# mLSTM rows by tile: denominators of four heads at once, and banks handed back before the statistics

## What is computed

```python
# for each of two directions d, per token j and head h:
den = s.sum(-1) + inter * einsum('bhck,bhcjk->bhcj', n_in, qc)
h   = num / maximum(abs(den), exp(-m_j))[..., None]
hx[0] + hx[1]                                    # both directions are added
(h - mu) * rsqrt(var + eps), merged, * ml_norm_w # then gated by sigmoid(o)
# attention: softmax(q k + bias, and q k over the context), times v
```

## Time and profile before

| | |
|---|---|
| median of 3 runs | 4099.18 us (4097.99 to 4102.63) |
| the profiled execution | 4098.68 us, of which its span is 4096.5 us |
| TensorE busy | 3561.6 us, 87% of the span |
| VectorE busy | 2733.5 us, 67% |
| rows and turns of layer 0 | from 363.56 us to about 472 us |
| rows and turns of layer 1 | from 2632.48 us |

### The profile page before, as it was taken

How to read it: one execution, slowest core, us unless ns; L and a number is a source line. 1 busy time by engine, 2 the same in 40 slices (tenths; PEclk the granted TensorE clock), 3 DMA queues, 4 the chain that set the end, 5 groups by cost and what they waited for, 6 DMA issues and landing times.

```text
span 4096.5 us, 46129 instructions
## 1 busy us (share of the span) xinstructions
PE 3561.6 (87%) x12012; PEld 1542.5 (38%) x12012; DVE 2733.5 (67%) x6918; ACT 1712.1 (42%) x4825; POOL 1846.6 (45%) x1405
## 2 busy tenths in 40 slices
PE   7998999888888888897888987899988888888887
PEld 3445654433333333333211221565433333333332
DVE  3106677677777777777766665768767777777775
ACT  2013534444444444444444443444444444444443
POOL 1111025556556555554433433104545655655555
PEclk9999999999999999999999999899999999999999
DMA  7653559999999999999999998658999999999998
GB/s 277 243 182 97 187 209 421 421 421 421 416 420 418 410 418 411 418 419 415 415 418 410 412 413 329 175 200 346 421 422 422 421 420 416 417 415 415 413 420 335
DMA packets 252758, 1503.73 MB, mean 367 GB/s; under 512 B 25888, under 2 KB 53024, under 8 KB 81808
## 3 DMA queue, kind: packets, MB, share of 16 engines
q0 software_dynamic: 193536, 1393.97, 83.4%
q1 hardware_dynamic: 59024, 107.45, 7.6%
HBM read 1494.91 MB, written 2.21 MB: 365 GB/s over the span
## 4 chain that ended last, share of the span: by engine, by line
DMA 44%; PE 27%; DVE 8%; issue 8%; ACT 7%; POOL 4%; SPq 1%; POOLq 0%; DVEq 0%; ACTq 0%
DMA arena<-in_updown,arena 44%; PE psum L1258 8%; POOL arena L1914 4%; DVE arena L2464 4%; PE psum L1201 3%; PE psum L1043 3%; PE psum L1059 2%; PE psum L1346 2%; ACT arena L1682 1%; PE psum L1071 1%; ACT arena L1678 1%; ACT L1748 1%; PE psum L1228 1%; ACT L1667 1%; PE psum L914 1%
## 5 line engine op out<-in xcount | busy, mean ns | idle before, releaser
L1914 POOL DMA_INDIRECT arena<-in_updown,arena x1280 | 1752.8, 1369 | 1751.3 <-PE psum L1258 845.4
L1258 PE MATMUL psum<-arena 128*128 128x512 f32 x4096 | 1998.0, 617 | 336.9 <-ACT arena L1682 320.2
L2464 DVE CUSTOM_DVE_ANT_0 arena<-arena 128x1024 bf16<-128x1024 f32 x1276 | 1566.0, 1227 | 901.3 <-DMA arena<-in_updown,arena 797.3
L1258 PEld LDWEIGHTS psum<-arena 128*128 128x128 f32 x4096 | 714.6, 191 | 1391.2 <-ACT arena L1682 826.5
L1748 ACT ACTIVATE arena<-arena 128x1 f32<-128x1 f32 x1280 | 259.1, 202 | 1663.1 <-DVE arena L2464 1660.2
L1682 ACT ACTIVATE arena<-CN,arena 128x128 f32<-128x128 f32 x1280 | 513.9, 402 | 44.9
L1678 ACT ACTIVATE arena<-arena 128x1 f32<-128x1 f32 x1280 | 376.7, 294 | 66.9 <-ACT arena L1748 3.9
L1346 PE MATMUL psum<-arena 64*64 64x512 f32 x2048 | 294.3, 647 | 117.9 <-ACT arena L1682 116.9
L1228 PE MATMUL psum<-arena 128*128 128x256 f32 (+1 forms) x1280 | 364.0, 385 | 3.0 <-ACT arena L1653 1.6
L1228 PEld LDWEIGHTS psum<-arena 128*128 128x128 f32 x1280 | 239.6, 191 | 260.6 <-issue 252.0
L1346 PEld LDWEIGHTS psum<-arena 64*64 64x64 f32 x2048 | 54.9, 136 | 306.8 <-ACT arena L1682 280.7
(11 more groups left out here) (266 smaller groups left out, 2644.6 us busy)
## 6 DMA issues: line engine op xcount, KB each, us to landing
arena<-in_ada_w POOLq DMA_DIRECT2D x40, 1024.0 KB, 5.7
arena<-in_updown,arena POOLq DMA_INDIRECT x1280, 14.7
arena<-in_wq SPq DMA_DIRECT2D x16, 1024.0 KB, 18.4
arena<-in_w_in SPq DMA_DIRECT2D x50, 256.0 KB, 7.3
arena<-in_w_in SPq DMA_DIRECT2D x5, 2048.0 KB, 12.8
arena<-in_w_in SPq DMA_DIRECT2D x17, 512.0 KB, 5.3
arena<-in_ada_w SPq DMA_DIRECT2D x4, 2048.0 KB, 14.2
arena<-in_consts SPq DMA_DIRECT2D x16, 512.0 KB, 5.7
```

The costliest lines, as they stand in the source:

```text
L1258: mm = e.matmul(ps[ACCUMULATORS[t % 2][hf]][:], diag[:, k % DIAGS, :], ring[k % RING][:, D + hf * 512:D + (hf + 1) * 512], start=first, st ...
L1914: e.indirect_dma_start(ring[k % RING], None, updown, bass.IndirectOffsetOnAxis(ap=idx16[:, k:k + 1], axis=0)).then_inc(sem(f"rows{k % RING ...
L2464: e.tensor_tensor_reduce(prod[:, k % 2, :], ring[k % RING][:, 0:D], u, 1.0, 0.0, ALU.mult, ALU.add, dots[:, k:k + 1]).then_inc(sem("expert ...
```

## The change

1. VectorE works by tile. `denominators(j)` waits until all four heads of tile j are in PSUM and does floor, maximum and reciprocal for four heads in one instruction each (three instead of eight). `head_rows(j, c)` adds up two heads' rows, `head_stats(j)` takes the four statistics of the tile afterwards.
2. The banks are handed back earlier: a new semaphore `mixer.sums_read` rises after the last reading of each pair of banks, ahead of the statistics. TensorE's group g waits for its value g - 1 (the same group g - 2). `keep_clock` and the turns wait for it too.
3. The first pairs' scores stand elsewhere: `scores(0)` after group 1, `scores(1)` after group 3 (both stood after group 2). Their maxima stand ahead of the last tile's denominators (they stood between its two groups), the divisions of pair 0 between its two halves of rows.
4. `no_bias` moves to other memory and is written before the rows; two of the eight bias blocks use a second block of zeros, `late_zeros`, which VectorE writes at p = 4 of the turns, after the wait for `mixer.bands_placed` that stood ahead of the first maxima.
5. Two semaphores of GpSimd (`ahead.ctx_copied`, `eps_set`) become one, with the counts adapted.

The diff, cut to its core:

```diff
@@ TensorE
-                        e.wait_ge(sem("mixer.h_done"), 2 * g - 2)
+                        e.wait_ge(sem("mixer.sums_read"), g - 1)
...
                 for g in range(2 * (NT - t0)):
                     head_sums(g)
-                    if g == 2:
+                    if g == 1:
                         e.wait_ge(sem("mixer.w_ready"), NT - t0)
-                        scores(0)
-                        scores(1)
+                    if g in (1, 3):
+                        scores(g // 2)
...
-                e.wait_ge(sem("mixer.h_done"), MLH * (NT - t0) - 2)
+                e.wait_ge(sem("mixer.sums_read"), 2 * (NT - t0) - 1)
                 keep_clock(ps[4], 3)
@@ VectorE
+                def denominators(j):
+
+                    e.wait_ge(sem("mixer.num_ready"), MLH * (j - t0 + 1))
+                    dn = psum[:, 4:4 + MLH, DV:2 * DV + 2:DV + 1]
...
+                    ch.link(e.scalar_tensor_tensor(out=den[:, MLH:2 * MLH, :], in0=dn, scalar=-1.0, in1=floor, op0=ALU.mult, op1=ALU.max))
+                    ch.link(e.tensor_tensor(den[:, 0:MLH, :], dn, den[:, MLH:2 * MLH, :], ALU.max))
+                    ch.link(e.reciprocal(rden[:], den[:, 0:MLH, :]))
+
+                def head_rows(j, c):
+
+                    heads = (2 * c, 2 * c + 1)
+                    for h in heads:
+                        ins = e.tensor_scalar(H[:, j, h * DV:(h + 1) * DV], psum[:, 4 + h, 0:DV], rden[:, h, 0:1], None, ALU.mult)
                     ch.link(ins)
+                    for h in heads:
+                        w = H[:, j, h * DV:(h + 1) * DV]
+                        ins = e.scalar_tensor_tensor(out=w, in0=psum[:, 4 + h, DV + 1:2 * DV + 1], scalar=rden[:, h, 1:2], in1=w, op0=ALU.mult, op1=ALU.add)
+                    ins.then_inc(sem("mixer.sums_read"), 1)
+
+                def head_stats(j):
+
+                    e.wait_ge(sem("mixer.sums_read"), 2 * (j - t0 + 1))
+                    for h in range(MLH):
+                        ins = e.bn_stats(bns[:, h, :], H[:, j, h * DV:(h + 1) * DV])
                     ch.link(ins)
...
+                    for h in range(MLH):
+                        e.bn_aggr(stat[:, j * MLH + h, :], bns[:, h, :]).then_inc(sem("mixer.h_done"), 1)
...
+                e.memset(no_bias, 0.0)
+                for j in range(t0, NT):
+                    if j == NT - 1:
+                        find_max(0)
+                        find_max(1)
+                    denominators(j)
+                    head_rows(j, 0)
+                    if j == NT - 1:
                         normalise(0)
                         normalise(1)
...
+                    head_rows(j, 1)
+                    head_stats(j)
+                    if j > t0:
+                        shift(j - 1)
                 for p in range(2, len(pairs) + 3):
...
+                    if p == 4:
+                        e.wait_ge(sem("mixer.bands_placed"), 16 * BAND_DMAS)
+                        ch.link(e.memset(late_zeros, 0.0))
```

More of the change, by code:

```diff
@@ L575, in build @@
         probT = [r(512) for _ in range(JOB_SLOTS - 1)] + [Region(ARENA_W - 512)(512)]
+        late_zeros_at = r.at
+        late_zeros = r(CTX)
+        assert r.at <= qe_at
+        r = Region(JOB_SLOTS * 512)
         nmax = r(JOB_SLOTS)
@@ L580, in build @@
         no_bias = r(CTX)
-        assert r.at <= qe_at and heads_top + KD * D >= lines_at
+        bns, den, rden = r(MLH, 6), r(2 * MLH, 2), r(MLH, 2)
+        assert r.at <= 4 * T and heads_top + KD * D >= lines_at
         def bias_group(n):
@@ L1027, in _ @@
                         if l and part == "c":
-                            e.wait_ge(sem("ahead.ctx_copied"), 2)
+                            e.wait_ge(sem("eps_set"), 5)
                         if i == 0 and part == "x":
@@ L1149, in turn @@
                         e.wait_ge(sem("mixer.bands_placed"), 16 * BAND_DMAS)
-                        e.wait_ge(sem("mixer.h_done"), MLH * (NT - t0) - 2)
+                        e.wait_ge(sem("mixer.sums_read"), 2 * (NT - t0) - 1)
                     if n == 2:
-                        e.wait_ge(sem("mixer.h_done"), MLH * (NT - t0))
+                        e.wait_ge(sem("mixer.sums_read"), 2 * (NT - t0))
                     bank = bank_for(("job", n))
@@ L1940, in _ @@
                     e.wait_ge(sem("ahead.u_kept"), 2 * KD + len(CTX_SECTIONS))
-                    e.tensor_copy(vml[:, 0, :, 0:DV], values_first[CTX_SECTIONS.index(COL_V)].rearrange("p (h d) -> p h d", h=MLH)).then_inc(sem("ahead.ctx_copied"), 1)
+                    e.tensor_copy(vml[:, 0, :, 0:DV], values_first[CTX_SECTIONS.index(COL_V)].rearrange("p (h d) -> p h d", h=MLH)).then_inc(sem("eps_set"), 1)
                     e.wait_ge(sem("experts.slot_done"), NT * PH * TOPK)
                     e.memset(clear_lines, 0.0).then_inc(sem("eps_set"), 1)
-                    e.tensor_copy(uTc[:, :, 0:P], u_first[:]).then_inc(sem("ahead.ctx_copied"), 1)
+                    e.tensor_copy(uTc[:, :, 0:P], u_first[:]).then_inc(sem("eps_set"), 1)
         @block.vector
@@ L2240, in _ @@
                     clear_scope(e, "experts.", ch)
[L2241 to L2252, removed]
-                    ch.link(ins)
[L2254 to L2258, removed]
-                    ch.link(ins)
[L2260 to L2267, removed]
@@ new lines, in _ @@
+                H, stat, rstd, _, shifts = heads_of[l]
+                def denominators(j):
+                    e.wait_ge(sem("mixer.num_ready"), MLH * (j - t0 + 1))
+                    dn = psum[:, 4:4 + MLH, DV:2 * DV + 2:DV + 1]
+                    o = (2 * NT + j) * 8
+                    v = gcol[:, o:o + 1]
+                    floor = bass.AP(v.tensor, v.offset, [v.ap[0], [1, MLH], [NT * 8 + 4, 2]])
+                    ch.link(e.scalar_tensor_tensor(out=den[:, MLH:2 * MLH, :], in0=dn, scalar=-1.0, in1=floor, op0=ALU.mult, op1=ALU.max))
+                    ch.link(e.tensor_tensor(den[:, 0:MLH, :], dn, den[:, MLH:2 * MLH, :], ALU.max))
+                    ch.link(e.reciprocal(rden[:], den[:, 0:MLH, :]))
@@ L2307, in keep_values @@
                     e.tensor_copy(dst, src).then_inc(sem("mixer.o_att"), 1)
-                groups = 2 * (NT - t0)
-                for g in range(groups):
-                    if g == groups - 1:
+                e.memset(no_bias, 0.0)
[6 more added lines that the diff above has]
+                    if j == NT - 1:
                         normalise(0)
                         normalise(1)
[L2313 to L2321, removed]
+                    head_rows(j, 1)
+                    head_stats(j)
+                    if j > t0:
+                        shift(j - 1)
                 for p in range(2, len(pairs) + 3):
```

12 lines of the change are left out of this document (6 added, 6 removed).

## The result

The changed kernel takes 4115.63 us (median of 7 runs, 4107.2 to 4117.7), the kernel before 4099.18 (7 runs, 4096.91 to 4102.63): a ratio of 1.0037, 95% interval 1.0027 to 1.0046. It is slower by 16.5 us. The profiled execution took 4115.64 us with a span of 4113.8.

A forecast was written before the change was run, and what follows sets the result against it. VectorE bounds the rows before; afterwards a mutual wait with TensorE over the banks, with a lasting clock fall, adds +12.5 in layer 0 and +1.5 in layer 1: +14.0 on 4098.68 gives 4112.7 us, range 4099 to 4117.

The forecast's parts named there:

- falls that last: Forecast case: TensorE drops to 1.2 GHz at the first 2.0 us idle piece until keep_clock; 4107 to 4117 us, chance 0.63.
- VectorE's work: Row tiles on VectorE: denominators 0.63, rows 2.5, statistics 1.25, shift 0.25; sum 4.6 us instead of 5.50.
- The wait: Between row tiles: TensorE and VectorE wait for each other over four banks; a tile costs 6.3 us, TensorE idle 2.0.
- The clock: TensorE during the rows: 2.0 us idle pieces bring 1.2 GHz, adding 3.3 us a tile, 3.0 for the first.
- the clock holds: Rival: TensorE keeps full clock through the rows; +2.4 in layer 0, -2.0 in layer 1, 4099.1 us; chance 0.18.
- Layer 0: Layer 0's stage, to pair 1's last copy: three tiles at half speed, keep_clock 4.2 us, end 420.2, +12.5 us.
- Layer 1: Layer 1's stage, to pair 1's last copy: one tile at half speed, end 2671.9, +1.5 us.
- The sum: Both layers' stages together: +14.0 us on the profiled 4098.68, giving 4112.7 us.
- Costs taken as nothing: Memsets of no_bias and late_zeros, moved bands_placed wait, later bias loads, merged semaphore: no cost; late_zeros 0.3 us a layer if uncovered.
- The places: Scores of pairs 0 and 1, 1 us each, lie in TensorE's idle time behind tiles 0 and 1.
- The idle times between groups: Skill section on PSUM cycling: short idle times between TensorE's groups swing the clock; by it the change lands at 4112.7.

The follow-up runs named there:

- the kernel with the clock held: Changed kernel plus two unread dense products on TensorE ahead of each tile from third to last but one, pair 1's scores later: 4104.8 us, ratio 1.0015.
- the kernel with the places undone: Changed kernel with scores, first maxima and divisions back where they stood before, whole-tile denominators and early hand-back kept: 4128.66 us, ratio 1.0078.
- the kernel with the wait alone: Kernel before with one line changed: a group's rows wait until both groups of their tile are in PSUM: 4138.44 us, ratio 1.0097.

## Why the prediction was right

Forecast 4112.7 us, range 4099 to 4117, the case "falls that last" on top; measured 4115.63.

- *VectorE's work.* Denominators 0.63 forecast, 380.37 - 379.73 = 0.64 measured; the 128x8 floor instruction takes 0.17, so from 2 to 8 elements a row the price goes with the instruction and not with its elements. Rows 2.5 against 2.45; a whole tile 4.6 against 4.53 with no wait in it.
- *The wait.* Hand-back after 1.9: 1.90. TensorE behind it by 0.1: 0.14. Tile 6.3: 379.73 - 373.35 = 6.38, and 6.4 in the kernel with the clock held. Idle time on TensorE 2.0: 2.0 to 2.1; on VectorE 1.7 and 5: 1.76 and 5.05. That VectorE would not wait ahead of the last `denominators` held for full clock only: it waited 2.37 us there, as the forecast's own numbers have it (VectorE free at 397.4 + 7.2 = 404.6, banks full at 407.0).
- *The clock.* A fall at the first piece of 2.0, lasting until keep_clock: so it came, without a recovery in the groups. That it came at the very first such piece was in part luck. In the kernel with the places undone it passed two such pieces, and the change's own seven runs go down to 4107.2 us, of which there is no trace. A tile at half speed 9.6: 389.41 to 399.09 is 9.68. The kernel with the dense products shows that the clock is what separates 4115.6 from 4104.8, which is where the rival "the clock holds" had put 4099.1. That rival's sum was too low in layer 0: +2.4 forecast, +3.5 measured, the difference being keep_clock, 4.27 us instead of 2.84, behind an idle piece of 2.77; layer 1 was -2.0 forecast and -0.5 measured. The rest of that kernel's 6.2 us lies outside the stages and is not explained.
- *Layer 0.* +12.5 forecast, +13.6 measured. Mis-sized is keep_clock: I put 4.2 us between 2.8 and 5.7, and it took 5.23. From scores(2) to the last copy 7.0 was forecast, 6.75 measured.
- *Layer 1.* +1.5 forecast, +0.8 measured: the clock fell some 1.2 us into the last tile's groups, so that tile took 8.7 and not 9.3 (6.3 + 3.0).
- *The sum.* Stages +14.0 forecast, +14.4 measured. The 2.1 (medians) to 2.9 us (spans) above that lie outside the stages, where the forecast had nothing, and stay open (see the result). That the total fits is also owed to layer 0's +1.1 and layer 1's -0.7 against the forecast.
- *Costs taken as nothing.* Nothing in the stage sums asks for more, and the turns behind them, with the memset of `late_zeros` and the wait in front of it, take 65.3 and 49.3 us with and without the change. The merged semaphore was not measured by itself.
- *The places.* The one thing the prediction undervalued: it put the scores of pairs 0 and 1 "in idle time" and left it there. The kernel with the places undone is 14.5 us slower. The scores stand where TensorE would otherwise wait, and the idle pieces ahead of tiles 1 and 2 are 1.22 and 1.01 us with them and 2.1 without; that this and not the maxima's new place makes the difference was not tested apart.
- *The idle times between groups.* The Trainium skill, "TensorE: Matmul & The Clock Gate", section "A second HAM failure mode: psum-queue depth-cycling", tells of a kernel that cycles through PSUM banks and whose clock swings between both levels because of short idle times between its groups. The traces agree in part: 0.50 granted over 33 us with pieces of 2.1 us in each tile. But there the clock did not swing, it stayed down, and with pieces of 0.8 us in each tile, just as frequent, it stayed at 1.00.

## What to carry to other kernels

Merging small instructions of a consumer saves their time only if the producer has a second place to write to: a joint wait over all buffers turns two overlapping engines into two that take turns, and the sum per step is then hand-back plus refill, whatever the consumer saved. Give the producer its second set of buffers first, and weigh the merge against the later start of the first step and against the producer's own work, which may bound then. Where TensorE must wait anyway between narrow products, let it run dense ones (worth 10.8 us here), or put real matmuls there.

## What the runs showed of the hardware that I had not expected

- TensorE stayed at 1.2 GHz for 34 us (381.4 to 415.5, from the granted clock of the first and last microsecond) although busy 79% of the time with products of 129 columns until keep_clock, and 47.8 us (378.5 to 426.3) in the kernel with the wait alone. Both ended during keep_clock's products of 512 columns. Shorter falls ended during pair scores of 256 columns, as in the earlier trace rows and at 374 us in the kernel with the places undone.
- Two dense products a tile, 2 us in 6.4, kept the clock at 1.00 in the same stretch.
- The same idle pieces of 2.1 us were not followed by a fall each time. The changed kernel fell at the first. The one with the places undone fell behind its first, came back with the pair scores, passed two more and fell at the fourth. The times of these two spread by 10.5 us (7 runs) and 9.4 us (5 runs), those of the kernel with the same wait and the clock held by 2.6 us (11 runs); but the kernel with the wait alone spread by only 4.1 us (4 runs), so this is a hint and no more.
